# Expert weights of the dense u stage multiplied over two token groups and two u tiles per instruction

## The chip, the cores and the metric

The kernel runs on one NeuronCore of a Trainium2 chip. The metric is the device time of one execution in microseconds (us); lower is better. Everything is float32.

## The reference, cut to what matters

A block of 512 tokens with 1024 features passes a mixer (an SSD branch and differential attention), which is not touched here, and then a channel mixer that retrieves experts by product keys. There, every token chooses 16 of 16384 experts in each of 8 heads, so 128 experts, each with a weight `g`:

```python
def block(xb):
    q = (xb @ w_q).reshape(tb, PEER_HEADS, 2, PEER_HALF)
    sc = einsum('thjd,hjnd->thjn', q, sub_keys)
    s_half, i_half = top_k(sc, K)                     # 16 rows i and 16 columns j
    ...
    idx = take_along_axis(cand_idx, top_pos, -1)      # i * 128 + j
    g = softmax(top_s, -1)
    h = gelu(einsum('td,thkd->thk', xb, u[idx]))
    return einsum('thk,thkd->td', g * h, v[idx])
```

`u` and `v` are tables of 16384 rows of 1024 floats (4 KB each).

## The kernel before, in words

After the mixer the two halves of the tokens take two different ways at the same time.

**Tokens 0 to 255 (the gathered half).** GpSimd (POOL) gathers one chosen row of `u` or `v` for each of 128 tokens with an indirect DMA (L1665, 512 KB each). VectorE (DVE) multiplies a row of `u` with the tokens and sums it (step `ru`, L1618), and adds a row of `v`, scaled by its weight, to the output (step `rv`, L1623). There are 256 rows of each kind. In the u stage a ring of five buffers (`UV`) holds the rows; GpSimd fetches the next row into a buffer when VectorE has used it (semaphore `used`).

**Tokens 256 to 511 (the dense half).** TensorE multiplies the whole tables. In the *u stage* (step `gl`, L929) tile j of 128 holds the 128 experts of column j, and eight accumulating multiplications, 16 records in the trace since a float32 product takes two passes, give a bank of 128 experts by 256 tokens. ScalarE (ACT) writes its GELU into `HBUF[:, j, :]` (L1195). In the *v stage* (L953) `HBUF` is the weight side of the products with 128 tiles of `v`. Between the two, each element of `HBUF` has to be multiplied by the weight that its token gives to its expert, or by zero. These weights are made during the second half of the u stage, in 64 groups of 4 tokens:

- step `oh` of group g: VectorE writes a one-hot of the expert rows (L1515), ScalarE one of the columns times the weight, with four `Abs` and four `Relu` (L1224, L1229), into one of two buffers.
- step `og` (L948): for each of the 4 tokens TensorE multiplies the two one-hots into bank `PS[4 + g % 4]`, which then holds weights of 128 rows by 128 columns by 4 tokens. It reuses the bank of group g - 4, so it waits for `gm_done` and `gc_done` of that group, and for the one-hots (`oh_i`, `oh_ja`).
- step `gm`: the columns j whose GELU is already in `HBUF` (`JS[g]` of them) are multiplied by VectorE at once (L1639, then `gm_done`). The weights of the columns still to come are copied by ScalarE from the bank into `HBUF` itself (L1205, then `gc_done`), behind a wait for `gm_done`.
- For a tile j that comes later, some weights then lie in `HBUF[:, j, 0:KW[j]]` already. ScalarE applies the GELU of these tokens in the bank (L1193) and that of the others into `HBUF` (L1195), then `ge_done`; step `gw` on VectorE multiplies `HBUF` by the bank for the first `KW[j]` tokens (L1643, then `gw_done`). Tile j uses bank `PS[(j + 2) % 4]`, so tile j + 4 waits for `ge_done` and `gw_done` of tile j (L924 to L926).

Every engine runs in its own order, and all orders come from one list, written by `work_order()`: its loop over j = 64 to 127 writes, for each tile, one `oh`, two or three rows (`rows(n)`), one `gm`, one `gl`, one `og` and one `gw`. An engine runs only its own steps of the list, in the list's order, so a step that waits holds up all that stands behind it on that engine. `JS` and `KW` are counted off from the list. The first three groups have their `gm` together, ahead of tile 67. The last steps of the kernel are four additions of the dense result on VectorE (step `fin`, L1649), which stand behind the last gathered row, and the stores of their halves.

## Time and profile before

| | us |
|---|---|
| three executions | 1399.74, 1400.70, 1405.98 |
| median | 1400.7 |
| profiled execution: span from first to last instruction | 1396.6 |
| median less that span | 4.1 |
| TensorE busy | 1364.6 (98%) |
| VectorE busy | 1083.6 (78%) |
| ScalarE busy | 435.3 (31%) |
| GpSimd busy | 610.1 (44%) |

No time of its own is given for the profiled execution besides its span; what lies around the span is taken as the 4.1 us by which the median exceeds it. The share of busy time is an average over stages with different limits. The granted clock of TensorE, as a fraction of full speed, averages 0.999 over the span.

### The profile page before, as it was taken

To read this page: it belongs to the slowest core of one execution; us is meant where nothing else is said; L and a number is where in the kernel's file an instruction comes from. 1 tells how busy PE (TensorE), PEld (TensorE's weight loads), DVE (VectorE), ACT (ScalarE), POOL (GpSimd) and SP (SyncE) were. 2 spreads that over 40 slices of the span, in tenths; PEclk is the share of its full clock that TensorE was granted. 3 is DMA by queue.
4 is the path that set the end of the run, shared out by engine and by line. 5 is a ranking of instruction groups with operands and counts; after the bars stand their busy time and mean duration, and the time that the engine had idled before them with its cause. 6 is when DMAs were issued, how large, how long until landed. Compare 5 with 4: busy or idle time off the path is not lost.

```text
span 1396.6 us, 16311 instructions
## 1 busy us (share of the span) xinstructions
PE 1364.6 (98%) x5402; PEld 933.1 (67%) x5402; DVE 1083.6 (78%) x2469; ACT 435.3 (31%) x1219; POOL 610.1 (44%) x516
## 2 busy tenths in 40 slices
PE   7999999999998999999999999999999999999998
PEld 5656648566587888888899999995444444444443
DVE  4535445899899999999999999998777677766656
ACT  2533532544411111112787887872000000000000
POOL 0000001733855444434466655664577645754440
PEclk9999999999999999999999999999999999999999
DMA  8322234975999999989899999999999999999997
GB/s 321 140 107 99 116 149 172 371 287 208 406 366 407 375 332 384 326 302 316 296 394 400 403 405 385 391 384 389 363 409 409 409 409 409 410 409 409 410 409 308
DMA packets 121763, 467.69 MB, mean 335 GB/s; under 512 B 13776, under 2 KB 14160, under 8 KB 115152
## 3 DMA queue, kind: packets, MB, share of 16 engines
q0 software_dynamic: 73728, 268.47, 49.9%
q1 hardware_dynamic: 47664, 197.66, 36.6%
q8 instruction: 43, 0.70, 0.2%
q10 hardware_dynamic: 288, 0.52, 0.1%
q14 instruction: 40, 0.33, 0.1%
HBM read 462.67 MB, written 3.93 MB: 334 GB/s over the span
## 4 chain that ended last, share of the span: by engine, by line
PE 60%; DMA 22%; DVE 9%; issue 3%; POOL 3%; ACT 2%; another core or an unknown queue 0%; DVEq 0%; SPq 0%; ACTq 0%; POOLq 0%
PE BANKS L929 32%; PE BANKS L729 11%; PE BANKS L721 9%; DMA BIG<-v,IDX 7%; DMA BIG<-u,IDX 7%; DMA UV<-v,IDX 4%; PE BANKS L948 4%; DMA UV<-u,IDX 2%; POOL BIG L1665 2%; DVE X L1623 1%; POOL UV L1665 1%; DVE BIG L1618 1%; DVE UV L1618 1%; DMA T<-away 1%; PE BANKS L912 1%
## 5 line engine op out<-in xcount | busy, mean ns | idle before, releaser
L1665 POOL DMA_INDIRECT UV<-u,IDX x153 | 184.1, 1203 | 411.1 <-DVE IDX L1495 263.3
L1665 POOL DMA_INDIRECT UV<-v,IDX x159 | 191.1, 1202 | 121.0 <-DVE X L1623 51.2
L1623 DVE SCALAR_TENSOR_TENSOR X<-UV,HG,X 128x1024 f32<-128x1024 f32 x159 | 203.9, 1282 | 40.7 <-DMA UV<-v,IDX 36.3
L929 PE MATMUL BANKS<-T 128*128 128x256 f32 x1024 | 229.2, 379 | 1.0 <-issue 1.0
L953 PE MATMUL BANKS<-T,BIG 128*128 128x512 f32 x512 | 225.2, 592 | 0.2 <-DMA T<-v 0.2
L953 PE MATMUL BANKS<-Y,BIG 128*128 128x512 f32 x512 | 225.1, 592 | 0.0
L929 PE MATMUL BANKS<-T,Y 128*128 128x256 f32 x992 | 221.9, 379 | 0.0
L1618 DVE SCALAR_TENSOR_TENSOR UV<-UV,Y 128x1024 f32<-128x1024 f32 x153 | 186.3, 1221 | 42.5 <-DMA UV<-u,IDX 37.7
L929 PEld LDWEIGHTS BANKS<-T 128*128 128x128 f32 x1024 | 192.0, 190 | 26.1 <-issue 1.4
L929 PEld LDWEIGHTS BANKS<-T,Y 128*128 128x128 f32 x992 | 186.0, 190 | 24.0
L953 PEld LDWEIGHTS BANKS<-Y,BIG 128*128 128x128 f32 x512 | 97.3, 190 | 122.5 <-issue 122.5
L953 PEld LDWEIGHTS BANKS<-T,BIG 128*128 128x128 f32 x512 | 97.1, 190 | 122.5 <-issue 121.5
L1665 POOL DMA_INDIRECT BIG<-v,IDX x97 | 116.9, 1205 | 122.5 <-DVE BIG L1618 55.5
L721 PE MATMUL BANKS<-T,BIG 128*128 128x256 f32 x736 | 164.1, 381 | 6.3 <-ACT BIG L1177 3.6
L729 PE MATMUL BANKS<-BIG,T 128*128 128x512 f32 x384 | 167.7, 593 | 2.1 <-DVE T L1256 1.5
L1665 POOL DMA_INDIRECT BIG<-u,IDX x103 | 117.8, 1143 | 101.2 <-DVE BIG L1618 49.6
L1623 DVE SCALAR_TENSOR_TENSOR X<-BIG,HG,X 128x1024 f32<-128x1024 f32 x97 | 124.7, 1285 | 41.7 <-DMA BIG<-v,IDX 37.0
L721 PEld LDWEIGHTS BANKS<-T,BIG 128*128 128x128 f32 x736 | 137.8, 190 | 28.1 <-issue 9.8
L1618 DVE SCALAR_TENSOR_TENSOR BIG<-BIG,Y 128x1024 f32<-128x1024 f32 x103 | 125.2, 1223 | 27.1 <-DMA BIG<-u,IDX 25.3
L729 PEld LDWEIGHTS BANKS<-BIG,T 128*128 128x128 f32 x384 | 71.9, 190 | 86.9 <-issue 86.7
L1186 ACT ACTIVATE HG<-HG 128x32 f32<-128x32 f32 x8 | 1.8, 230 | 341.8 <-DVE HG L1626 341.7
L1229 ACT ACTIVATE X<-X,KT 128x128 f32<-128x128 f32 x256 | 105.0, 485 | 0.0
(272 smaller groups left out, 1243.6 us busy)
## 6 DMA issues: line engine op xcount, KB each, us to landing
T<-u_t SPq DMA_DIRECT2D x64, 512.0 KB
T<-v SPq DMA_DIRECT2D x64, 512.0 KB
Y<-v SPq DMA_DIRECT2D x64, 512.0 KB
Y<-u_t SPq DMA_DIRECT2D x62, 512.0 KB
BIG<-w_in SPq DMA_DIRECT2D x23, 1024.0 KB, 4.8
BIG<-w_q SPq DMA_DIRECT2D x16, 1024.0 KB, 6.9
BIG<-w_out SPq DMA_DIRECT2D x8, 1024.0 KB, 4.9
UV<-v,IDX POOLq DMA_INDIRECT x159
```

The source lines that it names most:

```text
L721: last = nc.tensor.matmul(bank[:, 0:HT], wt, src[:, c, :], start=(c == 0), stop=(c == KC - 1))
L729: last = nc.tensor.matmul(bank[:, :], T8[:, b // 2, c, b % 2 * P:(b % 2 + 1) * P], wt, start=(c == 0), stop=(c == KC - 1))
L912: last = nc.tensor.matmul(bank[:, k * P:(k + 1) * P], Q2[:, q_at(half, hj), b * P:(b + 1) * P], KEYS[:, hj, :] if half or c < 2 else KEYS_ ...
L929: last = nc.tensor.matmul(PS[(i + 2) % 4][:, 0:HT], ub[:, c, :], T8[:, 1, c, :], start=(c == 0), stop=(c == KC - 1))
L948: last = nc.tensor.matmul(bank[:, :, k], ONEHOT[:, i % 2, 0, k, :], ONEHOT[:, i % 2, 1, k, :], start=True, stop=True)
L953: return nc.tensor.matmul(PS[4 + 2 * t + n][:, :], HBUF[:, j, t * P:(t + 1) * P], STREAM[j % NS][:, n * HALF:(n + 1) * HALF], start=(j == ...
L1186: nc.scalar.activation(HG[:, i % 2, :], HG[:, i % 2, :], ACT.Gelu).then_inc(gelu_done, 1)
L1229: last = nc.scalar.activation(ONEHOT[:, i % 2, 1, k, :], ONEHOT[:, i % 2, 1, k, :], ACT.Relu, bias=KT3[:, 2, t:t + 1], scale=KT3[:, 3, t:t ...
L1618: stt(row, row, 1.0, Y[:, n // 4, :], ALU.mult, ALU.mult, accum_out=acc).then_inc(used, 1)
L1623: stt(xb, row, HG[:, n % 2, i % UNIT:i % UNIT + 1], xb, ALU.mult, ALU.add).then_inc(used, 1)
L1665: pool.indirect_dma_start(row_place(s), None, u if kind == "ru" else v, bass.IndirectOffsetOnAxis(IDX[:, b, c:c + 1], 0)).then_inc(row_in[ ...
```

## The change

Two groups of tokens, g and g + 1 with g even, lie in two neighbouring banks (4 and 5, or 6 and 7), and two tiles, j and j + 1 with j even, too (2 and 3, or 0 and 1). `gm` now takes two groups in one VectorE instruction and in one ScalarE copy, `gw` two tiles in one VectorE instruction. `work_order()` writes a loop of 32 pairs of tiles in place of 64 tiles, with the same gathered rows in the same sequence. The first two pairs of groups have their `gm` together, now ahead of tile 68.

```diff
-    g = 0
-    for k, j in enumerate(range(FIRSTJ, NKEY)):
-        if 0 < g < NGRP - 1:
-            o += on("oh", g + 1)
+    for j in range(FIRSTJ, NKEY, 2):
+        g = j - FIRSTJ
+        o += on("oh", g + 1) if g else []
         o += rows(1)
-        if k >= 3:
-            o += [("gm", n) for n in range(max(0, g - 3), g) if ("gm", n) not in o]
+        if g == 4:
+            o += on("gm", 0)
+        o += on("gm", g - 2) if g >= 4 else []
         o += on("gl", j) + on("og", g)
-        g += 1
-        if k == 2:
-            o += on("sel", 1)
-        o += on("gw", j - 1)
-        o += rows(1 + (k % 4 == 0))
-    o += on("gm", NGRP - 1) + on("gw", NKEY - 1)
+        o += on("gw", j - 2) + rows(1)
+        o += on("sel", 1) if g == 2 else []
+        o += on("oh", g + 2) if g + 2 < NGRP else []
+        o += rows(1) + on("gl", j + 1) + on("og", g + 1) + rows(1 + (g % 4 == 0))
+    o += on("gm", NGRP - 2) + on("gw", NKEY - 2)
...
+        def by_group(g, first, end):
+
+            return HBUF[:, first:end, g * NTOK:(g + 2) * NTOK].rearrange("p j (a t) -> p j a t", t=NTOK)
+
+        def group_banks(g, first, end):
+            return BANKS[:, 4 + g % 4:6 + g % 4, :].rearrange("p a (j t) -> p j a t", t=NTOK)[:, first:end]
...
                     if i >= 4:
                         pe.wait_ge(ge_done, i - 3)
                         if KW[i - 4]:
-                            pe.wait_ge(gw_done, WEIGHED[i - 4] + 1)
+                            pe.wait_ge(gw_done, WEIGHED[(i - 4) // 2 * 2] + 1)
...
                     if i >= 4:
-                        pe.wait_ge(gm_done, i - 3)
-                        if i - 4 in COPIED:
-                            pe.wait_ge(gc_done, COPIED[i - 4] + 1)
+                        pe.wait_ge(gm_done, (i - 4) // 2 + 1)
+                        if (i - 4) // 2 * 2 in COPIED:
+                            pe.wait_ge(gc_done, COPIED[(i - 4) // 2 * 2] + 1)
...
-                    act.wait_ge(gm_done, i + 1)
-                    nc.scalar.activation(HBUF[:, JS[i]:NKEY, i * NTOK:(i + 1) * NTOK],
-                                         PS[4 + i % 4].rearrange("p (j t) -> p j t", t=NTOK)[:, JS[i]:NKEY, :],
-                                         ACT.Copy).then_inc(gc_done, 1)
+                    act.wait_ge(gm_done, i // 2 + 1)
+                    nc.scalar.activation(by_group(i, JS[i], NKEY), group_banks(i, JS[i], NKEY), ACT.Copy)\
+                        .then_inc(gc_done, 1)
...
                 elif step == "gm":
-                    dve.wait_ge(gb_full, i + 1)
+                    dve.wait_ge(gb_full, i + 2)
                     dve.wait_ge(ge_done, JS[i])
-                    hb = HBUF[:, 0:JS[i], i * NTOK:(i + 1) * NTOK]
-                    tt(hb, hb, PS[4 + i % 4].rearrange("p (j t) -> p j t", t=NTOK)[:, 0:JS[i], :], ALU.mult)\
-                        .then_inc(gm_done, 1)
+                    hb = by_group(i, 0, JS[i])
+                    tt(hb, hb, group_banks(i, 0, JS[i]), ALU.mult).then_inc(gm_done, 1)
                 elif step == "gw" and KW[i]:
-                    dve.wait_ge(ge_done, i + 1)
-                    tt(HBUF[:, i, 0:KW[i]], HBUF[:, i, 0:KW[i]], PS[(i + 2) % 4][:, 0:KW[i]], ALU.mult).then_inc(gw_done, 1)
+                    dve.wait_ge(ge_done, i + 2)
+                    hb = HBUF[:, i:i + 2, 0:KW[i]]
+                    tt(hb, hb, BANKS[:, (i + 2) % 4:(i + 2) % 4 + 2, 0:KW[i]], ALU.mult).then_inc(gw_done, 1)
```

`JS` and `KW` are counted in pairs accordingly, and the waits of the v stage ask for the same groups as before.

VectorE at the first weights, before: the three `gm` (L1639) stand right behind row `ru` 107 (the first instruction shown). L1515 is step `oh`, L1618 and L1623 are rows, L1500 to L1632 step `w` (the softmax and the weights of a unit of gathered rows).

```order
L1618 SCALAR_TENSOR_TENSOR UV,H<-UV,Y 128x1024 [waits row_in4]
L1639 TENSOR_TENSOR BIG<-BIG,BANKS 128x67x4 [waits ge_done,gb_full] x3
L1623 SCALAR_TENSOR_TENSOR X<-UV,HG,X 128x1024 [waits used,row_in0]
L1515 TENSOR_TENSOR X<-CONST,KT3 128x512 [waits gb_full]
L1618 SCALAR_TENSOR_TENSOR UV,H<-UV,Y 128x1024 [waits row_in1]
L1500 TENSOR_REDUCE SMALL<-G 128x2 [waits g_exp]
L1501 RECIPROCAL SMALL<-SMALL 128x2 [waits dve_seq]
L1502 TENSOR_TENSOR G<-G,SMALL 128x32 [waits dve_seq]
L1632 TENSOR_TENSOR HG<-G,HG 128x32 [waits gelu_done,dve_seq]
L1639 TENSOR_TENSOR BIG<-BIG,BANKS 128x68x4 [waits ge_done,gb_full,dve_seq]
L1643 TENSOR_TENSOR BIG<-BIG,BANKS 128x12 [waits ge_done]
```

The same place with the change (L1623 is now `ru`, L1628 `rv`, L1520 `oh`, L1505 to L1637 `w`, L1644 `gm`, L1648 `gw`):

```order
L1623 SCALAR_TENSOR_TENSOR UV,H<-UV,Y 128x1024 [waits row_in4]
L1628 SCALAR_TENSOR_TENSOR X<-UV,HG,X 128x1024 [waits used,row_in0]
L1520 TENSOR_TENSOR X<-CONST,KT3 128x512 [waits gb_full]
L1623 SCALAR_TENSOR_TENSOR UV,H<-UV,Y 128x1024 [waits row_in1]
L1505 TENSOR_REDUCE SMALL<-G 128x2 [waits g_exp]
L1506 RECIPROCAL SMALL<-SMALL 128x2 [waits dve_seq]
L1507 TENSOR_TENSOR G<-G,SMALL 128x32 [waits dve_seq]
L1637 TENSOR_TENSOR HG<-G,HG 128x32 [waits gelu_done,dve_seq]
L1644 TENSOR_TENSOR BIG<-BIG,BANKS 128x68x8 [waits ge_done,gb_full,dve_seq]
L1644 TENSOR_TENSOR BIG<-BIG,BANKS 128x68x8 [waits ge_done,gb_full]
```

The first multiplication has moved behind one `rv`, one `oh`, one `ru` and one `w`; TensorE's `og` of group 4, which needs it, has not moved.

ScalarE at the same place, before: the first copies (L1205) stand ahead of the GELU of tile 67.

```order
L1229 ACTIVATE X<-X,KT3 128x128 [waits oh_abs] x4
L1205 ACTIVATE BIG<-BANKS 128x61x4 [waits selt_done,used,idx_ready,gm_done,sc_away,chosen]
L1205 ACTIVATE BIG<-BANKS 128x61x4 [waits gm_done] x2
L1193 ACTIVATE BANKS<-BANKS 128x12 [waits hd_full]
L1195 ACTIVATE BIG<-BANKS 128x244
L1224 ACTIVATE X<-CONST,KT3 128x128 [waits gb_full]
```

With the change (L1229 and L1234 are now the `Abs` and `Relu`, L1211 the copy, L1199 and L1201 the GELU):

```order
L1201 ACTIVATE BIG<-BANKS 128x256 [waits hd_full]
L1229 ACTIVATE X<-CONST,KT3 128x128 [waits gb_full]
L1229 ACTIVATE X<-CONST,KT3 128x128 x3
L1234 ACTIVATE X<-X,KT3 128x128 [waits oh_abs] x4
L1211 ACTIVATE BIG<-BANKS 128x60x8 [waits selt_done,used,idx_ready,gm_done,sc_away,chosen]
L1211 ACTIVATE BIG<-BANKS 128x60x8 [waits gm_done]
L1199 ACTIVATE BANKS<-BANKS 128x16 [waits hd_full]
```

The copies now stand behind the GELU of tile 67 and the one-hots of group 5. The orders of TensorE, GpSimd and the DMA queue of SyncE are the same in both kernels, but for one wait of TensorE for `gw_done` that falls away.

## Rows read from the trace of the kernel before

**Rows 1.** The page: busy time by engine, and the chain that ended last.

```profile
PE 1364.6 (98%) x5402; PEld 933.1 (67%) x5402; DVE 1083.6 (78%) x2469; ACT 435.3 (31%) x1219; POOL 610.1 (44%) x516
...
PE 60%; DMA 22%; DVE 9%; issue 3%; POOL 3%; ACT 2%; another core or an unknown queue 0%; DVEq 0%; SPq 0%; ACTq 0%; POOLq 0%
```

**Rows 2.** Busy time by stretch: PE, PEld, DVE, ACT, POOL, clock, DMA share, GB/s.

```profile
675.00:692.40 17.40, 17.40 (x98) 15.77 (x98) 15.14 (x26) 13.45 (x36) 9.63 (x8) 1.00 0.78 280
692.40:949.90 257.50, 257.50 (x1426) 233.12 (x1425) 240.54 (x378) 203.25 (x660) 158.29 (x134) 1.00 1.01 395
949.90:1390.00 440.10, 439.76 (x1025) 194.15 (x1023) 304.64 (x541) 9.61 (x15) 233.82 (x203) 1.00 1.01 399
```

**Rows 3.** Waits, 690 to 954 us: who waited for whom, us in total, times, longest.

```profile
ACT BIG L1205 <- DVE BIG L1639: 55.1, 50, 3.4
...
DVE X L1623 <- DMA UV<-v,IDX: 10.4, 15, 1.7
DVE UV L1618 <- DMA UV<-u,IDX: 5.3, 11, 1.9
```

**Rows 4.** Timeline at the end of the kernel.

```profile
1382.79 7.03 PE L953 MATMUL BANKS<-Y,BIG 128*128 128x512 f32 x16
...
1389.01 1.28 DVE L1623 SCALAR_TENSOR_TENSOR X<-UV,HG,X 128x1024 f32<-128x1024 f32 x1
...
1390.21 2.47 DVE L1649 TENSOR_TENSOR X<-X,BANKS 128x512 f32<-128x512 f32 x4
```

**Rows 5.** Timeline of VectorE, first weights: start, us, instruction [idle before].

```profile
689.88 1.23 DVE L1618 SCALAR_TENSOR_TENSOR UV<-UV,Y 128x1024 f32<-128x1024 f32 x1 [1.86 <-DMA UV<-u,IDX]
...
691.03 1.12 DVE L1639 TENSOR_TENSOR BIG<-BIG,BANKS 128x268 f32<-128x268 f32 x3
692.06 1.28 DVE L1623 SCALAR_TENSOR_TENSOR X<-UV,HG,X 128x1024 f32<-128x1024 f32 x1
...
693.86 1.22 DVE L1618 SCALAR_TENSOR_TENSOR UV<-UV,Y 128x1024 f32<-128x1024 f32 x1
...
695.87 0.44 DVE L1639 TENSOR_TENSOR BIG<-BIG,BANKS 128x272 f32<-128x272 f32 x1
696.23 0.16 DVE L1643 TENSOR_TENSOR BIG<-BIG,BANKS 128x12 f32<-128x12 f32 x1
```

**Rows 6.** Timeline at the end of the u stage.

```profile
948.87 1.05 PE L948 MATMUL BANKS<-X 128*128 128x128 f32 x8
...
952.38 0.68 DVE L1639 TENSOR_TENSOR BIG<-BIG,BANKS 128x512 f32<-128x512 f32 x1
...
953.30 1.28 DVE L1623 SCALAR_TENSOR_TENSOR X<-UV,HG,X 128x1024 f32<-128x1024 f32 x1
```

**Rows 7.** Groups of VectorE instructions, 690 to 954 us.

```profile
L1639 DVE TENSOR_TENSOR BIG<-BIG,BANKS 128x268 f32<-128x268 f32 (+30 forms) x64 | 35.0, 549 | 0.1
L1643 DVE TENSOR_TENSOR BIG<-BIG,BANKS 128x12 f32<-128x12 f32 (+60 forms) x61 | 17.3, 283 | 0.0
```

**Rows 8.** Timeline of ScalarE: the first copies.

```profile
691.57 0.98 ACT L1205 ACTIVATE BIG<-BANKS 128x244 f32<-128x244 f32 x3 [3.40 <-DVE BIG L1639]
```

**Rows 9.** Timeline of TensorE: products `og` of groups 3 and 4.

```profile
688.07 1.05 PE L948 MATMUL BANKS<-X 128*128 128x128 f32 x8
...
692.42 1.05 PE L948 MATMUL BANKS<-X 128*128 128x128 f32 x8
```

**Rows 10.** Timeline around group 8: VectorE, ScalarE, and TensorE's `og` of groups 10, 11.

```profile
718.50 0.45 DVE L1639 TENSOR_TENSOR BIG<-BIG,BANKS 128x292 f32<-128x292 f32 x1
...
720.75 1.64 ACT L1229 ACTIVATE X<-X,KT 128x128 f32<-128x128 f32 x4
...
718.50 1.05 PE L948 MATMUL BANKS<-X 128*128 128x128 f32 x8
...
722.84 1.05 PE L948 MATMUL BANKS<-X 128*128 128x128 f32 x8
```

**Rows 11.** A stretch of the v stage: PE and PEld busy, clock, DMA share, GB/s.

```profile
1100.00:1150.00 50.00, 50.00 (x118) 22.20 (x117) 1.00 1.03 409
```

More of the change, by code:

```diff
@@ L418, in block_program @@
                 JS[i] = done[0]
-                done[1] += 1
-        WEIGHED = {j: n for n, j in enumerate(j for j in range(NKEY) if KW[j])}
-        COPIED = {g: n for n, g in enumerate(g for g in range(NGRP) if JS[g] < NKEY)}
+                done[1] += 2
+        WEIGHED = {j: n for n, j in enumerate(j for j in range(0, NKEY, 2) if KW[j])}
+        COPIED = {g: n for n, g in enumerate(g for g in range(0, NGRP, 2) if JS[g] < NKEY)}
         kind_of = lambda n: 2 if n >= NUNIT else int(n >= LATE)
@@ L429, in block_program @@
         rows_until = lambda step: sum(s[0] in ("ru", "rv") for s in ORDER[:POS[step]])
-        FIRST_V = rows_until(("gm", NGRP - 1))
+        FIRST_V = rows_until(("gm", NGRP - 2))
         def spaces():
@@ L960, in v_products @@
                 return last
-            pe.wait_ge(gm_done, NGRP - 2)
+            pe.wait_ge(gm_done, NGRP // 2 - 1)
             pe.wait_ge(gc_done, sum(g < NGRP - 2 for g in COPIED))
@@ L966, in _ @@
                 v_products(j, 0)
-            pe.wait_ge(gm_done, NGRP)
+            pe.wait_ge(gm_done, NGRP // 2)
             pe.wait_ge(gc_done, len(COPIED))
```

## The prediction

> **What bounds the kernel now.** I read the page first: TensorE is busy 98% of the span and holds 60% of the chain that ended last [rows 1]. A share over all stages doesn't tell what one stage is limited by, so the stretches come next [rows 2]. From 675 us to the last product of the u stage at 949.9 us TensorE is busy in every microsecond (17.40 of 17.40, 257.50 of 257.50), and in the v stage in 439.8 of 440.1. The reader should see that the changed steps lie beside a TensorE without any idle time. So VectorE's time can't be turned into time of the kernel there; only a wait of TensorE can change its end.
>
> VectorE is close behind: 240.5 of 257.5 us busy [rows 2], 17.0 us idle, most of it waits for gathered rows (10.4 and 5.3 us) [rows 3]. ScalarE has room: it waited 55.1 us for `gm` alone [rows 3]. The DMA engines move 395 GB/s in the stage and 399 in the v stage [rows 2].
>
> The end of the kernel has two feeders. TensorE's last record ends at 1382.79 + 7.03 = 1389.82 us. The last gathered row starts at 1389.01 and holds VectorE until the four `fin` begin at 1390.21; they run one behind the other and end at 1392.68 [rows 4]. After TensorE's end one `fin` of 0.68 us is all that is needed (four take 2.47, so about 0.6 from start to start), so TensorE may end 1392.68 - 1389.82 - 0.7 = 2.2 us later before the kernel does. A slip of the rows moves the end in full.
>
> **The change part by part.**
>
> *Fewer instructions.* `gm` goes from 64 to 32 instructions on VectorE, `gw` from 61 to 30. The elements stay the same. From 272 to 512 elements a `gm` grows from 0.44 to 0.68 us [rows 5, 6], 1.0 ns per element; the one of 272 starts 0.36 us before the next instruction [rows 5], so about 0.09 us is the cost of the instruction itself. 63 x 0.09 = 5.7 us of VectorE are freed, out of 35.0 + 17.3 = 52.3 us for the two steps [rows 7]. On the path to the end this is worth nothing: rows come in step with the tiles, `oh` and `gm` wait for TensorE, and TensorE is full. The cover is TensorE; were it gone, the 5.7 us would be the most to gain. The freed time turns into waits for rows or for TensorE. ScalarE's 32 fewer copies fall into its 55.1 us of waiting and are worth nothing either.
>
> *Reading two banks in one instruction.* No row of this kernel shows it. The order of elements is now 4 of one bank, 4 of the other, and so on. Below it costs nothing more than now, since HBUF was already read in pieces of 4 and gave the 1.0 ns per element [rows 5, 6]; above I take each paired element at twice the time, 52.3 us more. I take zero, being nearest to the rows that hop every 4 elements, and keep the other end for a rival. The Trainium skill, in "Vector Engine (DVE) Microarchitecture Reference", section 5.2, says that a port streams at full rate as long as it finds runs of two or more adjacent words, and that any hop between such runs is free; by it the term is zero, by the upper bound the sum would rise by 25 us (third rival). The trace agrees for SBUF; for two banks of PSUM nothing here shows it.
>
> *The first weights come later.* This is the term of the sum. Before, `gm` of groups 0 to 2 started at 691.03 us, right behind a gathered row [rows 5], ScalarE copied at 691.57 [rows 8], and `og` of group 4, which reuses the bank of group 0, started unhindered at 692.42 [rows 9]. Now the first `gm` stands behind an `rv`, an `oh`, a `ru` and a `w`. In the trace these go from 692.06 to 695.87, 3.81 us [rows 5]. If the row of that `rv` is there at once, `gm` starts at 691.03 + 3.81 = 694.84; if it comes only when it was used before, at 695.87. A row had just been waited for (1.86 us at 689.88) [rows 5], so I take the middle, 695.35. The pair has 544 elements: 0.44 + 0.272 = 0.71 us. Three old copies of 244 elements took 0.98 us [rows 8], so the copy of 480 takes at most two thirds of it, 0.65, say 0.6. `og` of group 4 can start at 695.35 + 0.71 + 0.6, with 0.03 for the signal: 696.7 us. TensorE stands 4.3 us, between 3.8 and 4.8. What is queued behind it is the rest of the u stage and the v stage; it never has idle time to catch up, so it ends at 1389.82 + 4.3 = 1394.1.
>
> *Shorter deadlines.* `og` of group g + 2 needs ScalarE's one-hots, queued behind the copy, which waits for `gm`. The tightest place before: `gm` of group 8 at 718.50, ScalarE's last `Relu` done at 720.75 + 1.64 = 722.39, `og` 11 at 722.84 [rows 10]: 0.45 us to spare, when `gm` lags 7.6 us behind the end of its `og` (718.50 less two periods of 4.34 plus 1.05 gives 710.87). A paired `gm` is 0.3 us longer there and the copy some 0.2, so 7.6 us is about the lag from which TensorE would wait again. But the stall of 4.3 us lets VectorE catch up: from some 7 us to 3. Likewise `gw` of a pair is now due two tiles after it can start, not three: 9.6 us (two periods of 4.34 and one `og` of 0.9) instead of 13.9, with 3 us of lag and 2 us of work. Cost of both: nothing, while the lag is below 7.
>
> *The end of the u stage.* The last `gm` now takes groups 62 and 63 together, so it waits for `og` 63, done before at 948.87 + 1.05 = 949.92 [rows 6], now at 954.2. The pair (1.1 us start to start) and `gw` (0.6) put the next gathered row at 955.9, against 953.30 [rows 6]. Rows slip by 2.6 us there. In the v stage the DMA moves 409 GB/s throughout [rows 11], so some or all of this stays to the end. GpSimd's own queue issues the same rows in the same order, and SyncE's queue is unchanged; each waits only as VectorE and TensorE do.
>
> **Sum.** TensorE's feeder: 4.3 - 2.2 (the time the last `fin` can absorb) = 2.1 us. The rows' feeder: 0 to 2.6 us. The later one counts: 2.1 to 2.6, I take 2.3. The span goes from 1396.6 to 1398.9; with the 4.1 us around it that is 1400.7 + 2.3 = 1403.0 us. About 0.5%, 7 us, is what a measurement of this kernel can tell from no change, so this is no change.
>
> **The rivals.**
>
> 1. *No stall, and the end's slack is used.* If the first pair comes in time after all, TensorE ends at 1389.82 as before, and if freed VectorE time also lets the rows end 2 us earlier, the last `fin` ends at 1390.5: 2.2 us less, 1398.5. For it: VectorE has 5.7 us less to do. Against: even the early bound of 694.84 is 2.4 us behind 692.42. Without the earlier rows it is 1400.7. Chance 0.14.
>
> 2. *The rows slip further.* At the end of the u stage VectorE stands idle for og 63 while landed rows wait, and each of the three rows in a row that it uses late is 0.52 MB at 409 GB/s, 1.3 us. Three such rows beyond the forecast give 4 us: 1407. For it: the v stage has no free DMA time. Against: the ring's five rows are landed then and are used quickly. Chance 0.13.
>
> 3. *Slower: VectorE becomes the bound.* Its place is every pair of tiles from 692 us on; its price is what a two-bank `gm` and `gw` cost above now. VectorE has 17.0 + 5.7 = 22.7 us of room in the stage, and the lag may grow from 3 to 7.6 us, 4.6 more, before `og` waits for the one-hots behind the copy. So it decides from 27.3 us of extra, about 1.5 times the present 52.3. If the whole doubles, 52.3 - 27.3 = 25 us: 1428. If only `gm` doubles, 35.0 - 27.3 = 8 us: 1411. For it: VectorE was idle only 7% of the stage. Against: the same pieces of 4 elements ran at full rate. Chance 0.08. By the skill's page above it would not happen, which is why the chance is not larger.
>
> That the change does not do what it says can be left out: the order holds 63 instructions fewer on VectorE.
>
> **How the numbers follow.** Forecast 0.65, rivals 0.14, 0.13 and 0.08. The range holds the forecast with its bounds (1402.5 to 1403.5 by the sum, and the spread of some microseconds that the three executions show), half of rival 1 and rival 2: 1399.5 to 1409. Faster by over 0.5% needs more than the 2.2 us that the end has to give: 0.02. Slower by over 0.5%: rival 3, and a tail of rival 2, 0.10. The rest, 0.88, lies within.
>
> **What would show it.** Right: TensorE idle once for about 4.3 us ahead of `og` of group 4, released by ScalarE's first copy at about 696.6 us, and no other idle time in the u stage; `gm` at a mean of about 1.0 us x32 and `gw` x30 at 0.5; VectorE's wait for rows or TensorE up by about as much as its busy time falls; `og` 63 ending near 954.2; the last `fin` close behind TensorE's end near 1394. Wrong: TensorE waiting at many groups (lag over 7), a paired `gm` of 1024 elements well above 1.2 us, or no idle time of TensorE at 692 us.

## The result, and the profile after

The changed kernel takes 1408.1 us (median of 10 executions, 1401.5 to 1412.0), the kernel before 1400.8 (10 executions beside it, 1399.2 to 1406.0): a ratio of 1.0048, 95% interval 1.0032 to 1.0065. By the ratio that is 6.7 us (the two medians are 7.3 apart), three times the 2.3 us of the forecast. It is still within 0.5%, but the interval leaves 1 out: the changed kernel is slower by a small amount that the measurement does tell from nothing. The profiled execution spans 1406.8 us, 10.2 more than the one before.

The page of the changed kernel, its busy times and the chain that ended last (before: [rows 1]):

```profile
PE 1371.3 (97%) x5402; PEld 937.2 (67%) x5402; DVE 1079.9 (77%) x2406; ACT 431.4 (31%) x1186; POOL 620.7 (44%) x516
...
PE 73%; DMA 9%; DVE 8%; issue 4%; POOL 3%; ACT 2%; another core or an unknown queue 0%; DVEq 0%; SPq 0%; ACTq 0%; POOLq 0%
```

TensorE is still the bound, yet no longer full. The windows of the u and v stages say where it stands idle; the columns are those of [rows 2]:

```profile
692.40:949.90 257.50, 251.66 (x1372) 226.38 (x1371) 224.76 (x307) 191.31 (x599) 158.00 (x127) 0.99 0.98 377
949.90:1390.00 440.10, 439.25 (x1058) 198.90 (x1057) 310.65 (x547) 16.29 (x38) 246.18 (x209) 1.00 1.02 404
```

In the u stage 5.8 us of 257.5 are idle, where before had none, and DMA moves 377 GB/s in place of 395. The 16 DMA engines are busy nearly all the time in both (share 0.98 and 1.01), so TensorE was not the only full resource here: I had noted the 395 GB/s and not asked how much room they leave. The waits from 690 to 970 us (waited for: us in total, times, longest):

```profile
DVE X L1628 <- DMA UV<-v,IDX: 16.6, 19, 2.1
DVE UV L1623 <- DMA UV<-u,IDX: 11.0, 13, 2.0
...
DVE X L1520 <- PE BANKS L954: 3.9, 4, 1.3
...
PE BANKS L954 <- ACT BIG L1211: 3.6, 1, 3.6
...
PE BANKS L935 <- DVE BIG L1648: 2.1, 4, 0.7
PE BANKS L935 <- ACT BIG L1201: 0.4, 1, 0.4
```

The one wait of 3.6 us for ScalarE's copy is the forecast one. The five for `gw` and the GELU were not forecast, nor that VectorE would wait 27.6 us for rows (15.7 before, in a stretch 16 us shorter, [rows 3]). TensorE's timeline (start, us, engine, line):

```profile
689.97 3.62 PE L935 MATMUL BANKS<-T 128*128 128x256 f32 x16
697.17 1.86 PE L954 MATMUL BANKS<-X 128*128 128x128 f32 x8 [3.59 <-ACT BIG L1211]
698.83 4.59 PE L935 MATMUL BANKS<-T 128*128 128x256 f32 x16
703.26 1.05 PE L954 MATMUL BANKS<-X 128*128 128x128 f32 x8
...
711.95 1.05 PE L954 MATMUL BANKS<-X 128*128 128x128 f32 x8
...
798.88 1.05 PE L954 MATMUL BANKS<-X 128*128 128x128 f32 x8
800.17 3.69 PE L935 MATMUL BANKS<-T 128*128 128x256 f32 x16 [0.23 <-DVE BIG L1648]
...
959.86 1.05 PE L954 MATMUL BANKS<-X 128*128 128x128 f32 x8
```

`og` of group 4 came at 697.17, 3.59 us late, and then took 1.86 us where it takes 1.05; tile 69 behind it took 4.59 where tile 68 had taken 3.62. The windows of TensorE alone (PE busy, PEclk, DMA share, GB/s) show why:

```profile
690.00:696.50 6.50, 3.59 (x18) 1.00 1.02 409
696.50:703.00 6.50, 5.83 (x23) 0.74 0.86 332
703.00:720.00 17.00, 17.00 (x96) 1.00 0.92 331
```

Right behind the wait the granted clock is 0.74 as a mean of 6.5 us, so part of that was at the lower of its two levels (1.2 of 2.4 GHz); before 696.5 and after 703 it is 1.00. That costs 0.8 + 1.0 = 1.8 us, which the forecast left out. Before, the clock was 1.00 over the same stretch.

VectorE's timeline shows the start of the chain, and how far `gm` lags behind its `og`:

```profile
691.75 1.28 DVE L1628 SCALAR_TENSOR_TENSOR X<-UV,HG,X 128x1024 f32<-128x1024 f32 x1 [1.50 <-DMA UV<-v,IDX]
...
695.62 1.35 DVE L1644 TENSOR_TENSOR BIG<-BIG,BANKS 128x544 f32<-128x544 f32 x2
706.15 0.73 DVE L1644 TENSOR_TENSOR BIG<-BIG,BANKS 128x560 f32<-128x560 f32 x1
714.85 0.75 DVE L1644 TENSOR_TENSOR BIG<-BIG,BANKS 128x576 f32<-128x576 f32 x1
798.86 0.90 DVE L1644 TENSOR_TENSOR BIG<-BIG,BANKS 128x720 f32<-128x720 f32 x1
965.24 1.22 DVE L1644 TENSOR_TENSOR BIG<-BIG,BANKS 128x1024 f32<-128x1024 f32 x1
```

`og` 7 ends at 711.95 + 1.05 = 713.00 and its `gm` starts at 714.85: 1.8 us of lag. `og` 25 starts at 790.19 and ends at 791.24, its `gm` starts at 798.86: 7.6 us. Some 95 us after the stall the lag is back where the forecast had the limit, and the waits begin: at groups 28, 32, 36, 48, 52, 55, 56, 60 and 62 a period from `og` to `og` is longer than normal, 4.6 us in sum (2.5 are the waits named above; the rest is short pauses beside them that the trace puts down to nothing). So 3.6 + 1.8 + 4.6 = 10.0 us: the difference in what I call **T**, the time from the start of `og` 3 to the start of `og` 63: 260.8 us before, 270.8 now.

The end of the kernel:

```profile
1394.45 7.03 PE L959 MATMUL BANKS<-Y,BIG 128*128 128x512 f32 x16
...
1399.17 1.28 DVE L1628 SCALAR_TENSOR_TENSOR X<-UV,HG,X 128x1024 f32<-128x1024 f32 x1
...
1400.37 2.47 DVE L1654 TENSOR_TENSOR X<-X,BANKS 128x512 f32<-128x512 f32 x4
```

TensorE's end moved from 1389.82 to 1401.48 (+11.7), the last row from 1389.01 to 1399.17 (+10.2), the last `fin` by the same 10.2 [rows 4]. The last additions came right behind the last row, as before.

### The profile page after: what moved, and what is told of

Same layout as the page of the kernel before. It is cut to its first block, busy times and chain, and to the rows that moved or that the text cites. A ratio compares the mean times of both kernels' runs of the same rounds, so it can differ in the third digit from the quotient of the medians.

```text
span 1406.8 us, 16184 instructions
## 1 busy us (share of the span) xinstructions
PE 1371.3 (97%) x5402; PEld 937.2 (67%) x5402; DVE 1079.9 (77%) x2406; ACT 431.4 (31%) x1186; POOL 620.7 (44%) x516
## 4 chain that ended last, share of the span: by engine, by line
PE 73%; DMA 9%; DVE 8%; issue 4%; POOL 3%; ACT 2%; another core or an unknown queue 0%; DVEq 0%; SPq 0%; ACTq 0%; POOLq 0%
PE BANKS L959 30%; PE BANKS L935 18%; PE BANKS L735 11%; PE BANKS L727 9%; DMA UV<-v,IDX 5%; DMA UV<-u,IDX 3%; POOL UV L1670 3%; DVE X L1628 2%; DVE UV L1623 1%; PE BANKS L918 1%; PE BANKS L954 1%; PE BANKS L707 1%; PE BANKS L851 1%; PE BANKS L762 1%; DVE BIG L1623 0%
## 5 line engine op out<-in xcount | busy, mean ns | idle before, releaser
L1670 POOL DMA_INDIRECT UV<-u,IDX x153 | 187.8, 1228 | 411.5 <-DVE IDX L1500 263.0
L1670 POOL DMA_INDIRECT UV<-v,IDX x159 | 197.1, 1239 | 124.0 <-DVE X L1628 54.0
L1628 DVE SCALAR_TENSOR_TENSOR X<-UV,HG,X 128x1024 f32<-128x1024 f32 x159 | 204.0, 1283 | 48.0 <-DMA UV<-v,IDX 42.4
L1623 DVE SCALAR_TENSOR_TENSOR UV<-UV,Y 128x1024 f32<-128x1024 f32 x153 | 186.4, 1222 | 46.2 <-DMA UV<-u,IDX 45.8
L1628 DVE SCALAR_TENSOR_TENSOR X<-BIG,HG,X 128x1024 f32<-128x1024 f32 x97 | 124.7, 1285 | 40.2 <-DMA BIG<-v,IDX 37.6
L1623 DVE SCALAR_TENSOR_TENSOR BIG<-BIG,Y 128x1024 f32<-128x1024 f32 x103 | 125.2, 1223 | 29.3 <-DMA BIG<-u,IDX 28.7
L1234 ACT ACTIVATE X<-X,KT 128x128 f32<-128x128 f32 x256 | 105.0, 484 | 0.0
```

The source lines that it names most:

```text
L1234: last = nc.scalar.activation(ONEHOT[:, i % 2, 1, k, :], ONEHOT[:, i % 2, 1, k, :], ACT.Relu, bias=KT3[:, 2, t:t + 1], scale=KT3[:, 3, t:t ...
L1623: stt(row, row, 1.0, Y[:, n // 4, :], ALU.mult, ALU.mult, accum_out=acc).then_inc(used, 1)
L1628: stt(xb, row, HG[:, n % 2, i % UNIT:i % UNIT + 1], xb, ALU.mult, ALU.add).then_inc(used, 1)
L1670: pool.indirect_dma_start(row_place(s), None, u if kind == "ru" else v, bass.IndirectOffsetOnAxis(IDX[:, b, c:c + 1], 0)).then_inc(row_in[ ...
```

## The experiments

Three theories stood against each other. **A:** VectorE lags because rows are used unevenly. Between two rows now stand steps for two groups or two tiles, the ring of five row buffers is given back in bursts, and time is lost in the stream of rows that nothing brings back; then TensorE waits for `gw`. **B:** each lost microsecond belongs to one moved deadline (the first pairs, the `gw` two tiles later), and undoing one returns its own part. **C:** the instruction over two banks costs more than two single ones.

T is worked out from timelines as above. The span is T + 1133.0 to 1136.0 us in every profile but two (1138.5 in e2, and e5, below), so T holds nearly the whole difference. Row distance is the mean and the standard deviation of the times between the starts of rows on VectorE within T; the mean is T in another form (some 134 rows in every kernel but e5 and e9), so only the deviation says something of its own. All columns but the last are of one profiled execution.

| kernel | T | span | wait for rows | row distance | median (before beside it), ratio and 95% interval |
|---|---|---|---|---|---|
| before | 260.8 | 1396.6 | 15.7 | 1.92, 0.33 | 1400.8 |
| before again (r1) | 267.1 | 1401.5 | 23.2 | 1.98, 0.41 | one execution, 1403.3 |
| changed | 270.8 | 1406.8 | 26.5 | 2.02, 0.64 | 1408.1 (1400.8) 1.0048, 1.0032 to 1.0065 |
| changed again (r2) | 272.2 | 1405.2 | 21.6 | 2.02, 0.61 | one execution, 1407.0 |
| e1 first pairs early | 268.0 | 1402.9 | 27.1 | 2.00, 0.53 | 1405.3 (1402.0) 1.0027, 1.0014 to 1.0040 |
| e2 instructions unpaired | 270.1 | 1408.6 | 17.6 | 2.01, 0.57 | 1410.4 (1402.0) 1.0062, 1.0041 to 1.0082 |
| e3 rows spread | 266.1 | 1401.7 | 20.1 | 1.97, 0.43 | 1405.9 (1402.0) 1.0024, 1.0012 to 1.0036 |
| e5 8 rows fewer | 269.2 | 1414.3 | 17.7 | 2.10, 0.71 | 1415.6 (1402.0) 1.0093, 1.0073 to 1.0113 |
| e4 = e1 + e3 | 264.7 | 1400.2 | 24.9 | 1.97, 0.41 | 1403.5 (1401.2) 1.0023, 1.0009 to 1.0038 |
| e4 again (r3) | 265.1 | 1398.7 | 23.4 | 1.95, 0.41 | one execution, 1400.7 |
| e7 e4, tiles single | 267.0 | 1400.9 | 24.5 | 1.98, 0.52 | 1403.4 (1401.2) 1.0016, 1.0004 to 1.0028 |
| e8 rows bunched | 274.2 | 1409.6 | 35.1 | 2.03, 0.73 | 1410.2 (1401.2) 1.0059, 1.0035 to 1.0082 |
| e9 e7 + 4 rows | 276.7 | 1411.2 | 31.6 | 2.01, 0.46 | 1410.4 (1401.2) 1.0058, 1.0036 to 1.0079 |
| e6 before, rows uneven | 267.6 | 1402.6 | 25.4 | 1.97, 0.43 | 1404.6 (1401.2) 1.0025, 1.0009 to 1.0041 |

(The wait for rows is taken from group 3 to group 62, hence 26.5 here and 27.6 above.)

Two things keep these columns from being read too finely. The unchanged kernel alone gives 260.8 and 267.1 us of T. And T starts at a point at which VectorE is not always equally far behind: the first `gm` came 6.5 us after the start of `og` 3 in the changed kernel's first profile and 11.1 us after it in its second. So the medians decide. If the intervals of two ratios are combined as those of independent measurements (my estimate), then against the changed kernel e3, e4 and e7 are faster, by 3.4, 3.5 and 4.5 us, each give or take 3; e1 is so at the very edge (2.9, give or take 2.9); e2 and e8 can't be told from it. e9 is slower than e7, by 5.9 give or take 3.4.

### Experiment e1: the first pairs early

```diff
-        if g == 4:
-            o += on("gm", 0)
-        o += on("gm", g - 2) if g >= 4 else []
+        o += on("gm", g - 2) if g > 4 else []
...
-        o += rows(1) + on("gl", j + 1) + on("og", g + 1) + rows(1 + (g % 4 == 0))
+        o += rows(1) + on("gl", j + 1) + on("og", g + 1)
+        o += on("gm", 0) + on("gm", 2) if g == 2 else []
+        o += rows(1 + (g % 4 == 0))
```

> Edit: the pairs of groups 0/1 and 2/3 are multiplied right behind the products of group 3, ahead of a gathered row, the one-hots, another row and the softmax step, so that the first wait of TensorE (3.6 us and 1.8 us behind it) should go. Measure: from the start of the weight products of group 3 to those of group 63, 260.8 us in the kernel before and 270.8 in the changed one. Theory A (the gathered rows set the pace: they are used unevenly, so one row takes 2.01 us on average where 1.93 is what TensorE's pace allows, and the early stall only gave slack that was used up later): the early wait goes, the later ones grow, 268 to 271 us in all, time within 2 us of the changed kernel. Theory B (two separate delays, the late start and the shorter deadlines): 265 us, the time 5 to 6 us below the changed kernel.

The timelines of ScalarE and TensorE:

```profile
691.18 1.12 ACT L1211 ACTIVATE BIG<-BANKS 128x480 f32<-128x480 f32 x2 [2.19 <-DVE BIG L1644]
...
692.75 1.05 PE L954 MATMUL BANKS<-X 128*128 128x128 f32 x8
```

`gm` now starts at 690.35 and `og` of group 4 at 692.75, right behind tile 68. The first wait is gone and with it the lower clock, 5.4 us. T fell only by 2.8, to 268.0: without a stall VectorE starts with a long lag and TensorE now waits more often later (periods too long by 7.2 us in sum). The median fell by some 3 us as well. The two stalls replace each other in part, as A has it; B, which adds them up, had T at 265 and the time 5 to 6 us down and is further off. A had a time within 2 us of the changed kernel's, and it is 2.8 lower, so that was not met either.

### Experiment e2: single instructions in the new order

```diff
-                    hb = by_group(i, 0, JS[i])
-                    tt(hb, hb, group_banks(i, 0, JS[i]), ALU.mult).then_inc(gm_done, 1)
+                    hb, gb = by_group(i, 0, JS[i]), group_banks(i, 0, JS[i])
+                    tt(hb[:, :, 0, :], hb[:, :, 0, :], gb[:, :, 0, :], ALU.mult)
+                    tt(hb[:, :, 1, :], hb[:, :, 1, :], gb[:, :, 1, :], ALU.mult).then_inc(gm_done, 1)
```

and the same for `gw` and the copies.

> Edit: the order and the waits of the changed kernel are kept, but each paired multiplication and copy is issued as two instructions again, one for each group or tile. Theory A (order of rows is the cause): no gain, 270 to 274 us from group 3 to group 63, since 63 instructions of 0.09 us come back on VectorE. Theory C (a read over two banks, or the length of one instruction, is the cause): 262 to 266 us, and the time 4 to 8 us below the changed kernel.

VectorE's groups, of this kernel from 690 to 970 us (busy, mean ns):

```profile
L1645 DVE TENSOR_TENSOR BIG<-BIG,BANKS 128x272 f32<-128x272 f32 (+30 forms) x32 | 17.7, 553 | 0.0
```

The other half of each pair (L1646) reads the same, 17.7. And of the changed kernel:

```profile
L1644 DVE TENSOR_TENSOR BIG<-BIG,BANKS 128x544 f32<-128x544 f32 (+30 forms) x32 | 30.5, 955 | 0.0
L1648 DVE TENSOR_TENSOR BIG<-BIG,BANKS 128x32 f32<-128x32 f32 (+29 forms) x30 | 12.6, 420 | 0.0
```

Paired, `gm` takes 30.5 us, in two instructions 35.4. Nothing is gained by going back: 1410.4 us, where C had it 4 to 8 us below the changed kernel. C falls, and the loss sits in the order of the steps and in the waits that pairs share, not in the instruction.

### Experiment e3: the same pairs, rows spread

```diff
-        o += on("gw", j - 2) + rows(1)
+        o += rows(1) + on("gw", j - 2) + rows(1)
...
-        o += rows(1) + on("gl", j + 1) + on("og", g + 1) + rows(1 + (g % 4 == 0))
+        o += on("gl", j + 1) + on("og", g + 1) + rows(1 + (g % 4 == 0))
```

> Edit: of the changed order, one gathered row is put between the multiplication by groups and that by tiles, so that the rows of a pair of tiles are used about 1.6 to 2.1 us apart, not 1.2 to 2.6; same number of rows. Theory A: mean distance of rows back to 1.92 to 1.95 us, no waits of TensorE after the first one: 266 us from group 3 to 63, time 3 to 5 us below the changed kernel. Theory B (the deadline of the multiplication by tiles is what fails): it now comes one row (1.2 us) later, so more waits: 271 us or more.

The waits from 684 to 958 us:

```profile
DVE X L1628 <- DMA UV<-v,IDX: 13.8, 25, 1.4
...
DVE UV L1623 <- DMA UV<-u,IDX: 7.7, 16, 1.0
...
DVE X L1520 <- PE BANKS L954: 5.6, 7, 1.9
...
PE BANKS L954 <- ACT BIG L1211: 3.4, 1, 3.4
```

`gw` comes a row later than in the changed kernel, and yet TensorE doesn't wait for it once: the first wait and its clock are all that is left, and T is 266.1. VectorE now waits more for TensorE (5.6 us; 3.9 in the changed kernel), and after the stall its lag stays at 1.7 to 4.9 us where it grew to 8.0. The time is lower too (1405.9). This is the run that speaks most for A, since B had `gw`'s deadline as a cause and this kernel makes it tighter. It does not clear the deadline altogether: VectorE enters with the slack of the first wait, and e4 below has the same spacing without it.

### Experiment e5: eight rows fewer in the u stage

```diff
-        o += rows(1) + on("gl", j + 1) + on("og", g + 1) + rows(1 + (g % 4 == 0))
+        o += rows(1) + on("gl", j + 1) + on("og", g + 1) + rows(1 + (g % 8 == 0))
```

> Edit: the changed order with 8 gathered rows fewer in the second half of the u stage (they follow in the v stage). Theory A: VectorE and the ring of rows have slack again, only the first wait of TensorE remains: 266 us from group 3 to 63; the 8 rows come back at the end at 1.3 us each, so the whole is 3 to 8 us slower than the changed kernel. Theory C (paired instructions): the later waits stay, 270 us.

TensorE's timeline:

```profile
698.09 2.05 PE L954 MATMUL BANKS<-X 128*128 128x128 f32 x8 [5.54 <-ACT BIG L1211]
699.93 5.38 PE L935 MATMUL BANKS<-T 128*128 128x256 f32 x16
```

With room on VectorE (17.2 us of waits for TensorE) all later waits are gone; the first is longer in this execution, 5.5 us, and the lower clock after it takes 1.0 + 1.8 = 2.8. The eight rows come back at the end: the span is T + 1145.1, some 10 us over the others. That is 1.3 us for each row, 0.52 MB at the 409 GB/s of the v stage [rows 11]. So the rows can't simply be moved out: the v stage is full. The run doesn't tell a VectorE with more room from DMA engines with more room, since eight rows fewer give both.

### Experiment e4: early and spread

Its edit is e1's and e3's together.

> Edit: the changed kernel with both order edits, the first pairs multiplied right behind the products of group 3, and one row between the multiplications by groups and by tiles. Theory A (uneven rows set the pace): the early wait of 5.3 us (3.6 us and the half clock behind it) and the later waits of 4.6 us both go; 261 to 263 us from the start of group 3's weight products to group 63's (260.8 before, 270.8 changed), time within 2 us of the kernel before. Theory B (the shorter deadline of the multiplication by tiles costs by itself, since VectorE starts with 7 us of lag here): waits of TensorE for that multiplication stay, 265 to 268 us.

TensorE's waits from 684 to 975 us, all of them:

```profile
PE BANKS L935 <- DVE BIG L1648: 2.1, 2, 1.4
```

264.7 us, and 265.1 in a second profile: A was 2 to 4 us too low, and what is left is the wait for `gw` at which B pointed (B's lower bound was 265). With VectorE 3.4 to 7.2 us behind from group 5 on, the spread rows do not keep it clear of that deadline. The median, 1403.5, is no better than e1's or e3's within the intervals.

### Experiment e7: groups paired, tiles single

```diff
-                    hb = HBUF[:, i:i + 2, 0:KW[i]]
-                    tt(hb, hb, BANKS[:, (i + 2) % 4:(i + 2) % 4 + 2, 0:KW[i]], ALU.mult).then_inc(gw_done, 1)
+                    tt(HBUF[:, i, 0:KW[i]], HBUF[:, i, 0:KW[i]], PS[(i + 2) % 4][:, 0:KW[i]], ALU.mult).then_inc(gw_done, 1)
```

with `gw` of j - 1 and of j behind the `og` of j and of j + 1.

> Edit: as the previous one, but only the groups are multiplied in pairs; the multiplication by tiles is one instruction per tile again, each behind its own tile's turn, with its deadline of three tiles. 30 instructions of 0.09 us come back. Theory A: rows 1.92 to 1.94 us apart, no wait of TensorE, 260.8 us from group 3 to 63, time equal to the kernel before, at most 2 us below it. Theory B: the same, but clearly better than the previous kernel (by 3 us or more); if both are equal, the deadline costs nothing once the rows are even.

TensorE still waits, now for one-hots:

```profile
PE BANKS L954 <- DVE X L1520: 2.1, 3, 1.4
```

The 260.8 without a wait did not come: T is 267.0. No wait for `gw` is left, but waits for one-hots stand in its place. In time e7 equals e4, so the `gw` due a tile earlier costs nothing that can be seen once the rows are even; where VectorE is late, TensorE waits for one of its steps or for another.

### Experiment e8: rows bunched

```diff
-        o += rows(1)
...
-        o += on("gw", j - 2) + rows(1)
+        o += on("gw", j - 2) + rows(3)
...
-        o += rows(1) + on("gl", j + 1) + on("og", g + 1) + rows(1 + (g % 4 == 0))
+        o += on("gl", j + 1) + on("og", g + 1) + rows(1 + (g % 4 == 0))
```

> Edit: the changed order with the rows of a pair of tiles used in one bunch of three and one of one or two (the opposite of the spread); same number. Theory A: the mean distance of rows grows beyond 2.04 us, since a ring of five buffers with a load of some 8 us stands empty after a bunch; TensorE waits more: 273 to 280 us from group 3 to 63, time 3 to 10 us above the changed kernel. Were VectorE's work alone the pace, nothing would change (270.8 us).

TensorE's waits for one-hots, from 684 to 975 us:

```profile
PE BANKS L953 <- DVE X L1519: 4.4, 6, 1.4
```

The waits for rows rise to 35.1 us, the largest of all, and T to 274.2, the way A says. That is 2 us over the changed kernel's second profile, less than two profiles of one kernel differ, and the time (1410.2) is above the changed kernel's with intervals that overlap. The run fits A and does not test it.

### Experiment e9: four rows more than e7

```diff
-        o += rows(1 + (g % 4 == 0))
+        o += rows(1 + (g % 4 == 0) + (g % 16 == 2))
```

> Edit: e7 with 4 gathered rows more in the u stage, so that the rows end 4 x 1.3 us earlier in the v stage if the DMA sets their pace there. If VectorE and the ring have room for them: no wait of TensorE in the u stage, its end unchanged, and the last additions no longer stand behind the last row: the time 2 us below the kernel before. If the ring has no room (rows at 1.92 us apart are its limit): TensorE waits again, 4 x 1.9 us less the 7 us of lag that it can take, so 0 to 3 us above e7.

```profile
DVE UV L1623 <- DMA UV<-u,IDX: 18.2, 25, 2.0
...
PE BANKS L954 <- DVE X L1520: 9.5, 12, 1.5
```

T rises by 9.7 us for four rows, 2.4 each, more than the distance of rows (2.0) and than the 1.3 us that one row takes of the DMA engines. If pairing had left room on VectorE that rows could use, they would have cost nothing. A miss: 0 to 3 us over e7 were expected, and it is 7.

### Experiment e6: the kernel before, with rows in twos

```diff
-        o += rows(1 + (k % 4 == 0))
+        o += rows(2 * (k % 2) + (k % 4 == 0))
```

Nothing is paired here: each second tile has its last row moved behind the next.

> Edit: the kernel before, unpaired and with its own deadlines and first group, but with the gathered rows moved between tiles: one row (sometimes two) behind an even tile's multiplications, and three with the odd tile, where it was two and two; same number. Theory A (uneven rows alone slow the stream of rows): VectorE's waits for rows rise from 15.7 us to 20 us or more, its lag no longer shrinks, and TensorE waits some: 262 to 268 us from the start of group 3's weight products to group 63's (260.8 before), the time 1 to 6 us above the kernel before. Were pairing or its deadlines needed for the slower stream: 260.8 us and no difference in time.

The waits from 684 to 958 us:

```profile
DVE X L1623 <- DMA UV<-v,IDX: 14.5, 22, 2.6
DVE UV L1618 <- DMA UV<-u,IDX: 11.2, 15, 1.8
...
PE BANKS L948 <- issue: 3.5, 4, 2.4
```

Unevenness alone, without one paired instruction, makes the kernel 3.5 us slower (1.0025, 1.0009 to 1.0041). The executions carry this, not the profile: T is 267.6, and the unchanged kernel's second profile has 267.1.

### Before, changed and e4 a second time

> The kernel before, unchanged, for a second profile: 260.8 us from group 3 to 63 within 1 us, VectorE's waits for rows within 3 us of 15.7. If they vary more, differences of some us in these numbers between other kernels are not to be read.

> The changed kernel, unchanged, for a second profile: 270.8 us from group 3 to 63 within 2 us, the first wait of TensorE at 3.6 us within 1 us.

> The kernel with both order edits (first pairs early, rows spread) for a second profile: 264.7 us from group 3 to 63 within 2 us. If it comes out at 261 to 262, its remaining 4 us were chance; if not, paired instructions cost the stream of rows something that even spacing does not give back.

The second profile of **before** differs from the first, on which the whole prediction was built (the waits from 684 to 955 us; PEld is TensorE's weight load):

```profile
DVE X L1623 <- DMA UV<-v,IDX: 12.0, 20, 2.0
DVE UV L1618 <- DMA UV<-u,IDX: 11.2, 15, 1.9
PEld BANKS L948 <- issue: 6.3, 10, 1.3
PE BANKS L948 <- issue: 2.3, 7, 1.0
...
PE BANKS L948 <- DVE X L1515: 0.7, 1, 0.7
```

Rows came later in this one (23.2 us of waits against 15.7), and the same kernel has T = 267.1 and TensorE waiting some 6 us in many small pieces. Before stands at the edge itself. Of the changed kernel, TensorE's timeline in the second profile:

```profile
697.72 2.04 PE L954 MATMUL BANKS<-X 128*128 128x128 f32 x8 [8.12 <-ACT BIG L1211]
699.55 4.11 PE L935 MATMUL BANKS<-T 128*128 128x256 f32 x16
```

The first wait is 8.1 us here, and only some 1.6 us come later; T is nearly the same (272.2 against 270.8). The row ahead of the first `gm` was waited for 2.38 us (1.50 in the first profile), but that is the smaller part: the `gm` stands at nearly the same time in both (696.17 and 695.62), and TensorE had reached `og` 3 4.0 us earlier. What I expected of r1 (T within 1 us, waits for rows within 3) and of the first wait in r2 (within 1 us) was missed; T in r2 and in r3 (265.1) came within 2 us as expected. So single values of T carry some 6 us of spread between executions for before, differences of a few us in them are not to be read, and the verdicts above lean on medians and intervals.

**Where a row's time goes.** The traces allow one more count, which none of the theories had used. If the indirect DMAs into the ring and the rows on VectorE are paired in their order, the times within T are (us, means; the last column is the median over the rows that VectorE stood waiting for):

| kernel | GpSimd starts the DMA to VectorE starts the row | VectorE ends the row to the buffer's next DMA | the first of these, rows waited for |
|---|---|---|---|
| before | 7.84 | 0.55 | 7.91 |
| before again (r1) | 8.16 | 0.50 | 8.34 |
| changed | 8.23 | 0.66 | 8.31 |
| changed again (r2) | 8.14 | 0.63 | 8.17 |
| e3 rows spread | 8.06 | 0.55 | 8.07 |
| e8 rows bunched | 8.21 | 0.76 | 7.90 |

With the 1.25 us that VectorE holds a buffer, a round of a buffer takes 7.84 + 1.25 + 0.55 = 9.64 us before and 10.14 changed, and a fifth of it is the row distance, 1.93 and 2.03. The ring is thus nearly as full as TensorE. Before, a row that was waited for had a round of 7.91 + 1.25 us and, in the median, 0.28 us until the buffer's next DMA: 9.44 us, so five buffers give a row each 1.89 us, and TensorE's pace asks for one each 1.93 (2.25 in 4.35 us; both are estimates from these figures). Of the 0.5 us by which the round grew, 0.11 lie in handing buffers back, where A has its cause (bunching adds 0.21), and 0.39 between the DMA's start and the row's. Rows waited for took 0.4 us longer to land, but so they did in r1 with nothing paired. How much of that comes from uneven use and how much from the DMA engines is not shown.

The DMA engines are the rival that no run tested. One tile of `u` and 2.25 rows, 0.52 MB each, are due every 4.35 us: 392 GB/s, where the most that a long stretch shows is 409 [rows 11]. The 17 GB/s between them bring one lost row back in some 31 us (both estimates). In T they move 394 GB/s in before, 384 in r1, 377 in both profiles of the changed kernel, and 386 in e3, at a busy share of 0.99 to 1.01 throughout. A kernel with fewer bytes and the same spacing of rows would tell the two apart.

## Why the prediction was right, and where it was not

The range (1399.5 to 1409) and "within 0.5%" held, with little to spare: the likeliest figure was 5 us too low. The mechanism of the main term was right. That the number stayed inside was the width of the range: the shorter deadlines, put at nothing, cost time, and the slack that was taken off the stall was not there. And 0.5% is not the least that can be told from no change here: with ten executions the interval is 0.33% wide, and it leaves 1 out.

- **Fewer instructions: worth nothing on the path.** Right in its place. `gm` and `gw` fell from 52.3 us to 43.1, by 9.2 rather than 5.7 (the part that overlaps the next instruction counts as busy too), and VectorE's waits rose by as much and more.
- **Two banks in one instruction: zero.** Right. 560 elements take 0.73 us and 1024 take 1.22. A straight line through all 32 paired `gm` gives 1.04 ns per element, one through the 64 single ones before 1.03. The rule of the Trainium skill ("Vector Engine (DVE) Microarchitecture Reference", section 5.2), that a hop between runs of two or more adjacent words, each on an 8-byte boundary, is free, stands there for SBUF; these times show the same for two alternating PSUM banks. Rival 3, VectorE as the bound through this price, falls: e2 is not faster.
- **The first weights come later: a wait of 4.3 us.** The mechanism was right, at the place named and with the releaser named: 3.6 us in this profile, 8.1 in r2, where VectorE was further behind TensorE when the first `gm` came due, and 5.5 in e5. Missing from the term was the clock: `og` 4 and tile 69 ran 1.8 us longer behind the wait, 1.5 in r2 and 2.8 in e5. Taking the first pairs early lowers the time by some 3 us, at the edge of what the intervals tell (e1).
- **Shorter deadlines: nothing, while the lag is below 7. This is the step that failed.** The condition was right and its premise was not: I took the lag of 3 us after the stall to stay. It was 1.8 us at group 7 and 7.6 at group 25, and from group 28 on TensorE waited, 4.6 us in all (1.6 in r2, where the stall had left more room). I had counted VectorE's work and not its supply. Busy time fell, but a row comes when a buffer has been handed back and filled; with steps of two groups and two tiles between rows, the distances between rows deviate by 0.64 us in place of 0.33, and in the first profiles the waits for rows grew by 11 us. (Not in the second ones: 23.2 us before, 21.6 changed.) What is shown by the times: unevenness without pairing costs 3.5 us (e6), and spreading the same rows over the same pairs gives about 3 back, with every later wait gone behind the stall (e3). Without the stall spreading leaves 4 us of T over before's first profile (e4, r3). Bunching points the same way within the noise (e8). That the cause is the handing back of buffers is argued; full DMA engines were not ruled out.
- **End of the u stage and sum.** TensorE may end 2.2 us later, I wrote, before the kernel does. That holds only if the rows stay put. They are used in step with TensorE's tiles, so every wait of TensorE moves them too, and the v stage, at 404 to 409 GB/s, never catches up: last row +10.2 us, `fin` +10.2, and span less T is constant to 3 us over nearly all kernels. So the 2.2 us that I took off the stall were not there to take, and a wait in the u stage should have been counted at its full price. From `og` 63 to the last row it took 440.1 us before and 439.3 now: no slip of 2.6 us was added at the last pair. Rival 1, no stall, did not happen. Rival 2 had nearly the right time (1407), but by luck: it had the rows slip at the end of the u stage, and they slipped over the whole second half of it.
- **The base.** "TensorE is busy in every microsecond" was true of that profile alone; r1 shows waits in the unchanged kernel. And 1.8 us lie around the profiled span (1.8 to 2.7 in the ten executions of the changed kernel), not the 4.1 I took by setting one span against the median of other executions; the forecast didn't hang on it.

What stays open is why the even and early version (e4, e7) is still some 2 to 3 us above before. Both have more waits for rows (23.4 to 24.9 us) than before's first profile (15.7) but hardly more than its second (23.2). No version was faster than before.

## What to carry to other kernels

Where VectorE both consumes a gathered stream and unblocks TensorE, spare time on VectorE is not slack unless the stream can fill it: look at the distances between consumptions and not only at busy time. After merging steps, spread the rest evenly between them. Work out the round of a buffer, from the start of its transfer to the start of the next, and set it against what the ring must give; and set the bytes due in a period against the fastest rate seen. And take two profiles of a kernel that sits at its limit before building a forecast on "no wait": here two of the same kernel differ by 6 us in one stage.

## What the runs showed of the hardware that was not expected

- TensorE's clock was lower behind single waits of 3.6, 5.5 and 8.1 us: 0.74, 0.58 and 0.69 as means of 6.5 us that begin 0.1 to 1.2 us before TensorE goes on. That cost 1.8, 2.8 and 1.5 us on top. Around the later waits of the changed kernel, up to 0.7 us each, it did not fall: it was 1.00 in every stretch of 6 us from 786 to 966.
- The same indirect DMA takes GpSimd 0.94 to 1.15 us in some cases and up to 1.9 in others. Its timeline in the changed kernel:

```profile
757.90 0.94 POOL L1670 DMA_INDIRECT UV<-v,IDX  x1 [0.30 <-issue]
759.43 1.14 POOL L1670 DMA_INDIRECT UV<-u,IDX  x1 [0.59 <-DVE X L1628]
...
771.18 1.91 POOL L1670 DMA_INDIRECT UV<-v,IDX  x1 [0.30 <-issue]
```

From 692.4 to 949.9 us 35 of 127 were long (over 1.5 us) in the changed kernel and 28 of 134 before. Before, 20 of the 28 long ones started within 0.4 us of the end of the one ahead, and 19 of the 106 others; in the changed kernel it was 13 of 35 and 41 of 92, so closeness doesn't explain them there. Whether they are a cause of late rows was not tried.
